# Differential attention: undivided shares combined, head sums by query, and the first four tiles of its output projection together

## What is computed

```python
def diff_attend(q, k, v, lam, lambda_init, subln_g):
    s = jnp.einsum('bqhtd,bkhtd->bthqk', q, k).astype(jnp.float32) * HEAD_DIM ** -0.5
    p = jax.nn.softmax(s, axis=-1)
    a = (p[:, 0] - lam * p[:, 1]).astype(v.dtype)
    o = jnp.einsum('bhqk,bkhe->bqhe', a, v)
    o = rms_norm(o, subln_g) * (1.0 - lambda_init)
    return o.reshape(o.shape[0], o.shape[1], DIFF_HEADS * 2 * HEAD_DIM)
# rms_norm(x, g) = x * rsqrt(mean(x * x) + 1e-6) * g
# behind it: out = o @ w_out, a gated residual, layer norm, a convolutional feed-forward layer
```

## Time and profile before

| | us |
|---|---|
| median of 3 runs | 1879.32 (1878.71 to 1881.64) |
| the profiled execution | 1878.08 |
| its span, first to last instruction | 1876.3 |
| PE busy in the span | 1750.7 (93%) |
| DVE busy | 1075.4 (57%) |
| ACT busy | 827.8 (44%) |
| mean granted TensorE clock | 0.951 |

### The profile page before, as it was taken

How to read it: one execution, slowest core, us unless ns; L and a number is a source line. 1 busy time by engine, 2 the same in 40 slices (tenths; PEclk the granted TensorE clock), 3 DMA queues, 4 the chain that set the end, 5 groups by cost and what they waited for, 6 DMA issues and landing times.

```text
span 1876.3 us, 24577 instructions
## 1 busy us (share of the span) xinstructions
PE 1750.7 (93%) x10048; PEld 1375.2 (73%) x10048; DVE 1075.4 (57%) x1616; ACT 827.8 (44%) x1186; POOL 0.9 (0%) x5
## 2 busy tenths in 40 slices
PE   5988999979999999999988999789999989999997
PEld 2744446657787787699468999789876957877775
DVE  2255665434433444543965666647766645888886
ACT  3334443433312332523535544445444325767664
POOL 0000000000000000000000000000000000000000
PEclk7999999989999999999888999889998877999998
DMA  9311334234333433323022464433322306989993
GB/s 357 121 34 46 113 113 157 90 112 179 138 121 139 175 133 125 134 90 113 1 73 104 154 206 160 160 112 135 113 91 90 123 12 261 364 326 354 339 332 133
DMA packets 42676, 287.72 MB, mean 153 GB/s; under 512 B 4784, under 2 KB 5936, under 8 KB 11200
## 3 DMA queue, kind: packets, MB, share of 16 engines
q1 hardware_dynamic: 42384, 285.97, 42.0%
q10 hardware_dynamic: 144, 0.06, 0.0%
q0 software_dynamic: 32, 0.07, 0.0%
HBM read 285.03 MB, written 1.05 MB: 152 GB/s over the span
## 4 chain that ended last, share of the span: by engine, by line
PE 83%; DVE 8%; ACT 5%; issue 2%; DMA 1%; SPq 0%; DVEq 0%; ACTq 0%
PE ps L481 17%; PE ps L482 16%; PE ps L483 16%; PE ps L2486 5%; PE ps L2456 2%; PE ps L2457 2%; PE ps L2460 2%; PE ps L1399 2%; DVE WL L471 2%; PE ps L517 2%; PE ps L2392 2%; DMA ring<-wts 1%; PE ps L1368 1%; PE ps L1300 1%; PE ps L597 1%
## 5 line engine op out<-in xcount | busy, mean ns | idle before, releaser
L481 PE MATMUL ps<-HH,WH 128*128 128x512 f32 (+2 forms) x1552 | 522.4, 337 | 36.7 <-DVE WL L471 23.2
L471 DVE TENSOR_TENSOR WL<-ring,WH 128x2048 fp32r<-128x2048 f32 (+2 forms) x191 | 413.3, 2170 | 172.0 <-ACT WH L461 171.6
L483 PE MATMUL ps<-HH,WL 128*128 128x512 f32 (+2 forms) x1552 | 510.7, 329 | 0.0
L482 PE MATMUL ps<-HL,WH 128*128 128x512 f32 (+2 forms) x1552 | 510.5, 329 | 0.0
L461 ACT ACTIVATE WH<-ring 128x2048 fp32r<-128x2048 f32 (+2 forms) x191 | 346.6, 1817 | 224.9 <-DMA ring<-wts 83.5
L481 PEld LDWEIGHTS ps<-HH,WH 128*128 128x128 f32 x1552 | 301.5, 194 | 88.8 <-issue 36.2
L483 PEld LDWEIGHTS ps<-HH,WL 128*128 128x128 f32 x1552 | 301.4, 194 | 23.3
L482 PEld LDWEIGHTS ps<-HL,WH 128*128 128x128 f32 x1552 | 301.9, 195 | 22.4 <-issue 0.5
L481 PE MATMUL ps<-parts,WH 128*128 128x512 f32 (+1 forms) x352 | 119.7, 340 | 0.0
L482 PE MATMUL ps<-parts,WH 128*128 128x512 f32 (+1 forms) x352 | 118.4, 336 | 0.0
L483 PE MATMUL ps<-parts,WL 128*128 128x512 f32 (+1 forms) x352 | 118.3, 336 | 0.0
(11 more groups left out here) (332 smaller groups left out, 2191.8 us busy)
## 6 DMA issues: line engine op xcount, KB each, us to landing
ring<-wts SPq DMA_DIRECT2D x206, 1024.0 KB, 5.0
arena<-wts SPq DMA_DIRECT2D x38, 1024.0 KB, 7.0
ring<-wts SPq DMA_DIRECT2D x32, 704.0 KB, 4.0
X<-xin SPq DMA_DIRECT2D x4, 512.0 KB, 9.5
cst<-csts SPq DMA_DIRECT2D x1, 1373.0 KB, 15.4
ring<-wts SPq DMA_DIRECT2D x3, 384.0 KB, 3.1
out<-arena SPq DMA_DIRECT2D x2, 512.0 KB, 2.9
ring<-wts SPq DMA_DIRECT2D x1, 640.0 KB, 3.5
```

The source lines that it names most:

```text
L471: e.tensor_tensor(lo, raw(i), hi.bitcast(F32), ALU.subtract).then_inc(*up("low", i))
L481: e.matmul(o, w[0][:, cols], x[0], start=k == 0, stop=False)
L482: e.matmul(o, w[0][:, cols], x[1], start=False, stop=False)
L483: return e.matmul(o, w[1][:, cols], x[0], start=False, stop=k == nk - 1)
```

## The change

1. The two maps are combined undivided: the row sums are kept in `share`, one scalar lam z0/z1 per query is formed, and one scalar_tensor_tensor per query tile replaces the two instructions of before. ACT takes both copies of the turned tile.
2. The head sums are formed by query: the squares are the stationary operand, a column of 1/128 the moving one, so that a sum lies in 128 partitions x 1 column for each query tile. Two groups, heads 0 to 5 and heads 6 and 7, have a bank, a limit (1e-6 z0 z0), a root and a reciprocal each; the first group's come in steps 9 and 10 of the loop. A dummy root at step 8 loads the table.
3. The spread takes the weight of a head, broadcast, as the stationary operand and the identity as the moving one, two matmuls of 128 columns a head. DVE makes the low part of head h - 1 after the scaling of head h.
4. The first four tiles of the projection are done together: for each k all four tiles, when `od_low` k has come. The norm's sums come later: the shift sums after tile 4, the spread of the shift after tile 5, moments 0 to 3 after tile 6, the rest after tile 7. `act_out` and `dve_out` stay as they are.
5. The low part of dout 1 is made in `dve_diff_inputs`, ahead of lambda.

```diff
+        def pe_out_four(e, key, src, arrive, n, tag):
+            bs = [[bank(e, "out", key, 2 * i + m) for m in range(2)] for i in range(2)]
+            four_tiles(e, [index[key + (i,)] for i in range(2)], [[ps[:, b, 0:n] for b in bi] for bi in bs], src,
+                       [key + (2 * i,) for i in range(2)], (arrive,))
+            for j in range(4):
+                banks.give(bs[j // 2][j % 2], "y", tag, j)
...
-            for i in range(8 // mt_per):
+            if four:
+                pe_out_four(e, key, src, arrive, n, tag)
+            for i in range(2 if four else 0, 8 // mt_per):
...
-                        pe_out_sums(e, N, j)
+                        for d in {4: (1,), 5: (2,), 6: (3, 4), 7: (5, 6, 7)}[j] if four else (j,):
+                            pe_out_sums(e, N, d)
...
+            act_high(e, index["dout", 0], 2)
             e.wait_ge(*at("lam.sums"))
...
             rope("kept.qd", Qd, 7)
+            dve_low(e, index["dout", 0])
             lv = V("lam", 0, 256)
...
         def pe_diff(e):
-            bank(e, "head_sums")
...
             pe_head_sum(e, 7)
-            e.wait_ge(*at("inverse.head"))
-            for h in range(8):
-                b = bank(e, "spread", h)
-                e.matmul(ps[:, b, 0:256], ident[0:8, h:h + 1].to_broadcast([8, 128]), SQ1[0:8, :], start=True,
-                         stop=True).then_inc(*up("spread", h))
-                banks.give(b, "od_unit", h)
+            for part in range(2):
+                e.wait_ge(*at("diff_weighed.head", part))
+                for h in HEADS[part]:
+                    b = bank(e, "spread", h)
+                    for qt in range(2):
+                        t = e.matmul(ps[:, b, 128 * qt:128 * qt + 128], weight[:, qt, h:h + 1].to_broadcast([128, 128]),
+                                     ident, start=True, stop=True)
+                    t.then_inc(*up("spread", h))
+                    banks.give(b, "od_unit", h)
...
+                    act_diff_turn(e, i - 2)
+                if i == 8:
+                    e.activation(small[:, 127:128], EPS6, ACT.Sqrt)
+                if i == 9:
+                    act_head_root(e, 0)
+            act_head_root(e, 1)
...
+        def act_diff_turn(e, j):
+            if j >= 2:
+                e.wait_ge(*at("diff_values", j - 2))
+            for qt in range(2):
+                e.wait_ge(*at("diff_turned", j, qt))
+                e.activation(*diff_turned(j, qt), ACT.Copy).then_inc(*up("diff_p", j, qt))
...
+        def dve_head_limit(e, part):
+            w, z = part_of(weight, part), part_of(share[:, 0, :, :], part)
+            e.scalar_tensor_tensor(out=w, in0=z, scalar=1e-6, in1=z, op0=ALU.mult,
+                                   op1=ALU.mult).then_inc(*up("diff_weighed.limit", part))
+            e.wait_ge(*at("head_sum", HEADS[part][-1]))
+            e.wait_ge(*at("diff_weighed.limit", part))
+            e.tensor_tensor(w, w, head_sums(part), ALU.add).then_inc(*up("diff_weighed.square", part))
...
+                if i == 9:
+                    dve_head_limit(e, 0)
+                if i == 10:
+                    dve_head_weight(e, 0)
+            dve_head_limit(e, 1)
+            for h in range(9):
+                if h < 8:
+                    if h == 1:
+                        dve_head_weight(e, 1)
+                    e.wait_ge(*at("spread", h))
+                    e.scalar_tensor_tensor(out=Qd[:, h, :], in0=Qd[:, h, :], scalar=sg, in1=B("spread", h)[:, 0:256],
+                                           op0=ALU.mult, op1=ALU.mult).then_inc(*up("od_unit", h))
+                if h:
+                    e.wait_ge(*at("od_high", h - 1))
+                    e.tensor_tensor(OD[1][:, h - 1, :], Qd[:, h - 1, :], OD[0][:, h - 1, :].bitcast(F32),
+                                    ALU.subtract).then_inc(*up("od_low", h - 1))
...
         def dve_diff_scale(e, j):
...
-            e.reciprocal(rv[:, cols], sm[:, cols]).then_inc(*up("diff_weighed.share", j, 0))
+            e.reciprocal(r, share[:, 1, :, j]).then_inc(*up("diff_weighed.share", j, 0))
...
-            e.tensor_scalar(es[:, cols], rv[:, cols], lm[:, 5:6], None, ALU.mult).then_inc(*up("diff_weighed.share", j, 1))
+            e.scalar_tensor_tensor(out=c, in0=r, scalar=lm[:, 5:6], in1=share[:, 0, :, j], op0=ALU.mult,
+                                   op1=ALU.mult).then_inc(*up("diff_weighed.share", j, 1))
...
-                e.tensor_scalar(P3[z][:, qt, :], P3[z][:, qt, :], es[:, i + 1:i + 2], None,
-                                ALU.mult).then_inc(*up("diff_weighed.second", j, qt))
-                e.wait_ge(*at("diff_weighed.second", j, qt))
-                e.scalar_tensor_tensor(out=PAD[:, z, qt, :], in0=PAD[:, z, qt, :], scalar=rv[:, i:i + 1],
-                                       in1=P3[z][:, qt, :], op0=ALU.mult, op1=ALU.add).then_inc(*up("diff_weighed", j, qt))
+                e.scalar_tensor_tensor(out=PAD[:, z, qt, :], in0=P3[z][:, qt, :], scalar=c[:, qt:qt + 1],
+                                       in1=PAD[:, z, qt, :], op0=ALU.mult, op1=ALU.add).then_inc(*up("diff_weighed", j, qt))
...
         def pe_head_sum(e, h):
+            part = int(h >= HEADS[1][0])
+            b = bank(e, "head_sums", part) if h == HEADS[part][0] else banks.of["head_sums", part]
             e.wait_ge(*at("diff_exp.square", h))
-            e.matmul(ps[0:8, banks.of["head_sums",], 0:256], C("strip8")[:, 7 - h:15 - h], SQ1, start=h == 0,
-                     stop=h == 7).then_inc(*up("head_sum", h))
...
+            for qt in range(2):
+                t = e.matmul(ps[:, b, 8 * qt + h:8 * qt + h + 1], SQ1[:, 128 * qt:128 * qt + 128], C("o128", 1), start=True,
+                             stop=True)
+            t.then_inc(*up("head_sum", h))
...
-            pe_out(e, ("dout",), 8, OD, lambda k: ("od_low", k), 256, 2, 1, "n10")
+            pe_out(e, ("dout",), 8, OD, "od_low", 256, 2, 1, "n10", four=True)
```

More of the change, by code:

```diff
@@ L962, in build @@
         lm, sg = small[:, 96:104], small[:, 104:105]
+        share = small[:, 128:160].rearrange("p (a q h) -> p a q h", a=2, q=2)
+        weight = small[:, 160:176].rearrange("p (q h) -> p q h", q=2)
         top[0] = ARENA - 16 * 256
@@ L1558, in act_diff, with part_of, head_sums, act_head_root @@
                 e.activation(OD[0][:, h, :], Qd[:, h, :], ACT.Copy).then_inc(*up("od_high", h))
+        def act_diff_turn(e, j):
[4 more added lines that the diff above has]
+                e.activation(*diff_turned(j, qt), ACT.Copy).then_inc(*up("diff_p", j, qt))
+        def part_of(rows, part):
+            return rows[:, :, HEADS[part][0]:HEADS[part][-1] + 1]
+        def head_sums(part):
+            return part_of(B("head_sums", part)[:, 0:16].rearrange("p (q h) -> p q h", q=2), part)
+        def dve_head_limit(e, part):
[5 more added lines that the diff above has]
+            e.tensor_tensor(w, w, head_sums(part), ALU.add).then_inc(*up("diff_weighed.square", part))
+        def act_head_root(e, part):
+            w = part_of(weight, part)
+            e.wait_ge(*at("diff_weighed.square", part))
+            e.activation(w, w, ACT.Sqrt).then_inc(*up("root.head", part))
+        def dve_head_weight(e, part):
+            w = part_of(weight, part)
+            e.wait_ge(*at("root.head", part))
+            e.reciprocal(w, w).then_inc(*up("diff_weighed.head", part))
         def dve_diff(e):
+            e.tensor_scalar(sg, V("subln"), 1.0 - LAM_INIT, None, ALU.mult).then_inc(*up("diff_weighed.gain"))
             for i in range(11):
@@ L1659, in pe_head_sum @@
         def pe_head_sum(e, h):
+            part = int(h >= HEADS[1][0])
+            b = bank(e, "head_sums", part) if h == HEADS[part][0] else banks.of["head_sums", part]
             e.wait_ge(*at("diff_exp.square", h))
-            e.matmul(ps[0:8, banks.of["head_sums",], 0:256], C("strip8")[:, 7 - h:15 - h], SQ1, start=h == 0,
-                     stop=h == 7).then_inc(*up("head_sum", h))
-            if h == 7:
-                banks.give(banks.of["head_sums",], "root.head")
+            for qt in range(2):
+                t = e.matmul(ps[:, b, 8 * qt + h:8 * qt + h + 1], SQ1[:, 128 * qt:128 * qt + 128], C("o128", 1), start=True,
+                             stop=True)
+            t.then_inc(*up("head_sum", h))
+            if h == HEADS[part][-1]:
+                banks.give(b, "diff_weighed.square", part)
         def act_diff_values(e, h):
```

38 lines of the change are left out of this document (7 added, 31 removed).

## The result

After: **1884.58 us** (median of 9 runs, 1882.45 to 1886.26) against 1879.44 before (9 runs on the same chip, 1878.24 to 1881.64). The ratio is 1.0027, 95% interval 1.0016 to 1.0037: slower, by 5.1 us. The forecast was 1884.0.

A forecast was written before the change was run, and what follows sets the result against it. PE and DVE both nearly full in the head loop. Four tiles end 13.5 us earlier, but the tail takes 28.7 instead of 14.3, plus 1.7 clock and 1.1 offset: +3.6; with 0.7 and 0.4, +4.7: 1884.0, range 1878.5 to 1890.

The forecast's parts named there:

- Undivided shares: Head loop: DVE loses 1.64 us a head, PE then bounds at 5.65 instead of 6.61; sixth value product 4.3 earlier.
- Head sums by query: Head loop, PE: four passes of the new head sums take 0.52 us, bounds 0.26 to 0.96, so nothing changes.
- Table load: End of the heads: the 1.28 us load leaves the path, the dummy root standing where ACT waits for DVE anyway.
- What falls due: Behind the four tiles: DVE's unchanged order makes PE wait 2.3 and 5.7 us; last y at T + 28.7, not T + 14.3.
- the two small clock terms: Added to the +3.6: 0.7 us for the clock after the short pause, 0.4 for a head loop longer at low clock.
- the forecast's third item: Projection's end: ACT's square 3 waits for moments 0, gate/up halves stand behind it; all serial, last y at T + 28.7.
- Clock behind the long pause: Tile 6, after PE's pause of 5.7 us: the clock falls to its low level and the tile loses 1.7.
- the early split: Start of the head loop: a 2.28 us DVE subtraction moved ahead of the lambda sums delays the first row maximum by 2.2.
- the eighth bank: Start of the head loop: head_sums no longer holds a bank, so head 1's fourth score needs no wait, about 0.9 us back.
- A: Rival, faster: DVE reaches the splits of dout 2 and 3 before PE needs them; about 1867 us; chance 8%.
- B: Rival, no visible change: PE keeps the full clock through both pauses and the loop; 1881.2 us; 32% with mis-sized small terms.
- C: Rival, slower still: low clock in the loop to about 922 costs 2 to 4 us, 1.7 more if spreads run low; 1889; 20%.

The follow-up runs named there:

- e6: The kernel before with the undivided shares alone, both turned copies on ACT, small term under the root left unscaled: 1875.68 us.
- e2: The changed kernel with the projection's tiles one by one again and without the early split of dout 1: 1865.78 us.
- e1: The changed kernel with the projection's tiles one by one again, the early split of dout 1 kept: 1866.41 us, ratio 0.9934.
- e10: The kernel of e2 without the dummy root at step 8, so the table load comes with the first group's root: 1865.03 us.
- e4: The changed kernel with DVE's low part of dout 3 made ahead of its wait for the spread of the shift: 1877.84 us.
- e8: The changed kernel, four tiles still together, with DVE's and ACT's order and PE's moments rearranged to suit them: 1868.08 us.
- e11: The changed kernel with 22 useless identity products on PE in its pause before the seventh tile: 1888.25 us.
- e7: The kernel before with the early split of dout 1, ahead of lambda, alone: 1886.36 us.
- e3: The changed kernel with DVE's low part of dout 2 made ahead of y0 and y1, while PE does the four tiles: 1882.42 us.
- e5: The kernel before with four tiles together, late norm sums and the early split of dout 1, old head loop and head norm: 1899.74 us.
- e12: The kernel of e8 with the low part of dout 1 made at step 9 of the head loop instead of ahead of lambda: 1864.78 us.

## Why the prediction was right

**By parts,** each run taken against before in its own batch: part 1 gives -4.2 (e6), parts 2 and 3 -10.3 (e2 less e6), part 5 +0.6 (e1 less e2), part 4 +19.0 (after less e1; 18.2 by the bare medians). They are steps of one chain, so they add up to the measured +5.1 by construction, and each price holds in this order only: in the loop of before, part 5 costs 6.5 and part 4 13.4. So some 14 of gain and 19 of loss hide behind a result of 0.27%.

**Step by step**, forecast against profiled execution:
- *Undivided shares.* 5.65 per head forecast, 5.68 measured; DVE has slack (its copy waits up to 1.3 for PE), and e6 shows the gain of part 1 alone. But the 0.44 on top of PE's own 5.21 lies elsewhere than forecast: the value product waits 0.25, not 0.87, for ACT's second copy in every other head, and 0.9 more is in the score products, which wait for ACT's exponentials. PE's own work is less by the shorter head sum. That the sum still gives 5.65 is partly luck.
- *Head sums by query.* 0.52 forecast from eight passes of the modulation, 0.50 measured. But the transposes start 0.36 behind it, where before they started 0.53 behind the head sum (942.25 and 942.78), so it wins 0.17 a head and isn't quite neutral.
- *Table load.* Priced at 1.28 off the chain, and so it is (941.22). By the Trainium skill (ScalarE: Activation LUTs, "What ACT_TABLE_LOAD costs") a switch costs 2.66, with a drain beside the load. Neither after nor e10 shows more than the 1.28: in both the root follows the load at once, and the measurement decides.
- *Spreads and start of the tiles.* 952.4 forecast, 952.63 measured; the end of the fourth tile 964.0 against 964.13.
- *What falls due.* Pauses 2.3 and 5.7 forecast, 2.09 and 5.66 measured; last y 995.5 forecast without the two small clock terms (0.7 and 0.4) and 996.6 with them, 994.99 measured. (The tail of before, put at 14.3, is 14.5 by the earlier trace rows.) e4 shows the cause of the second pause by removing it, and e8 shows that the order is nearly the whole loss. The 16.4 are made of these pauses, 1.8 of clock, 6.4 behind PE's last tile (the serial halves of gate/up, the forecast's third item) and 0.4 of small steps.
- *Clock behind the long pause.* 1.7 forecast; the seventh tile took 984.12 - 979.44 = 4.7 instead of 2.9, that is 1.8. e11, where PE is kept busy and the clock stays at 1.00, shows that PE's idleness is what brings it. The short pause was taken at 0.4 x 1.7; in the profiled execution of after it cost nothing, in that of e11 1.4 up to the spread of the shift.

**What was mis-sized,** in amounts that cancelled: the early split was put at 2.2 less 0.9 for the eighth bank. Counted from the scores' start, it costs 3.7 at head 1 (25.2 in after, 21.5 in e2) and 3.2 in the old loop (e7), of which 2.1 is PE's longer pause and 1.65 value product 0, which falls in a low phase of the clock in after (3.61; e7 similar) and not in e2 (1.96). On the other side parts 2 and 3, the bank among them, win 2.6 there (24.1 in e6, 21.5 in e2), not 0.9. The net at head 1 is 1.0 later than forecast, and the last three heads, 4.12 apart instead of 4.30, with a shorter end behind them (7.2 instead of 7.8), gave that back. In a kernel with the old loop the same step would have been wrong by 4 us (e7).

**How much of the number is luck.** The forecast put all of its +4.7 into the stage. There the profiled executions show +3.0; 1.0 more is in the rest, where nothing was forecast, and 1.0 is that the medians differ by more than the profiled spans. The mechanism and the sizes of its large terms are shown; that +4.7 meets +5.1 so closely is in part chance.

**The rivals.** A (splits come in time) is what e8 builds by hand, at 1868.1 against its 1867: the mechanism was rightly priced, but without a new order it doesn't happen. B (full clock everywhere) fell with the 0.50 over 979 to 983. C (low clock longer in the loop) did not decide: 0.96 over 909 to 937.

**Open.** The price of the early split in the new loop lies between 0.6 (e1, e2 by time) and 3.6 (by stage). Whether part 4 also lengthens the rest (885.4 to 887.3 in after, e3, e4, e8 and e11, but 882.8 and 883.4 in e5 and e12, 882.3 to 884.9 in the others) isn't settled. What the low clock costs in time alone was not isolated.

## What to carry to other kernels

When one engine's steps are fused (four tiles, whose ends all come together), list what the other engines did between the old ends. Each of those works has lost its cover, and a wait in their queues that used to be short now holds everything behind it. Move that work with the fusion, or leave the fusion out: here a single line (e4) was worth 6.7 us and undoing a single call 18.2. And time the parts of a combined change alone. This one read as "a little slower" and held a kernel 0.7% faster than before.

## What the runs showed of the hardware

- A pause of 2 to 3 us on PE may or may not cost the full clock. The same pause of 2.65 left it at 1.00 before and was followed by 0.64 and 0.51 in e7 and by 0.50 over 948 to 950 in e5. The same 2.09 left it at 1.00 in after (966 to 971) and e4 (969 to 973), and was followed by 0.66 over 966 to 971 in e11 and over 985 to 990 in e5. After the pauses of 4.7 to 5.7 that were looked at the low level followed each time (0.61 behind the 4.87 and 0.50 behind the 5.66 of after, 0.50 over 976 to 982 around the 5.62 of e3, 0.57 over 998 to 1003 around the 5.63 of e5, 0.66 behind the 4.72 of e7). A single profiled execution doesn't tell which outcome is the usual one.
- Identical code ahead of the stage ended between 888.8 and 892.2 in 14 profiled executions. Comparing stretches by their own start, not by absolute positions, made e2, e4 and e7 readable.
